# Pool products, early modulation products and output weight splits moved within the attention stage of a two-layer backbone step

## The reference

```python
q, k, v, p = split(h @ w_in)                       # 4 heads of 2 x 64, pool input p of 512
s = einsum('bhqjd,bhkjd->jbhqk', qblk, k) * 64 ** -0.5
pr = softmax(s, axis=-1)
a = pr[0] - lam * pr[1]                            # differential attention
o = einsum('bhqk,bhkv->bhqv', a, v)
o = o * rsqrt(mean(o * o) + LN_EPS) * norm_g * (1 - lam_init)
mixed = einsum('btgc,gcd->btgd', centred_window_means(p), pool_w)   # 4 groups
out = concat([o, mixed * pool_scale]) @ w_out
x = LN(alpha * x + gate * out)
```

## Time and profile before

| | |
|---|---|
| median of 3 runs | 1456.0 us (1455.67 to 1458.06) |
| the profiled execution, its own time | 1456.0 us |
| its span, first to last instruction | 1454.4 us |
| TensorE busy | 1373.7 us, 94% of the span |
| TensorE weight loads | 1129.6 us, 78% |
| VectorE busy | 887.6 us, 61% |
| ScalarE busy | 725.8 us, 50% |
| mean granted TensorE clock | 0.985 |

### The profile page before, as it was taken

The page is one execution under the profiler, slowest core; times in us unless marked ns, Lnnn a source line. Parts: engine busy times, 40 slices in busy tenths (PEclk is TensorE's granted clock), DMA queues, the critical chain, the costliest instruction groups (busy, mean ns, idle before and its releaser), DMA issues.

```text
span 1454.4 us, 20841 instructions
## 1 busy us (share of the span) xinstructions
PE 1373.7 (94%) x6944; PEld 1129.6 (78%) x6944; DVE 887.6 (61%) x1184; ACT 725.8 (50%) x1123; POOL 213.5 (15%) x280
## 2 busy tenths in 40 slices
PE   6999889999999999998889899999999999999986
PEld 2766468999999879986567588888888888888874
DVE  1325557363333484224876697655555999999977
ACT  1323555322333353323434685445445888888863
POOL 1010000070000004103420644100000700000110
PEclk9999999999999999999989999999999999999998
DMA  9786673369443424446655699766656999999991
GB/s 349 227 306 226 217 231 113 116 238 330 131 127 122 129 58 133 116 173 222 235 196 176 235 381 352 253 191 217 206 180 184 369 369 366 371 367 371 370 371 61
DMA packets 254102, 341.24 MB, mean 235 GB/s; under 512 B 15886, under 2 KB 209708, under 8 KB 253900
## 3 DMA queue, kind: packets, MB, share of 16 engines
q1 hardware_dynamic: 241354, 299.55, 62.8%
q0 software_dynamic: 12432, 40.70, 7.5%
q10 hardware_dynamic: 242, 0.01, 0.0%
HBM read 318.13 MB, written 21.02 MB: 233 GB/s over the span
## 4 chain that ended last, share of the span: by engine, by line
PE 80%; DVE 8%; DMA 3%; ACT 3%; issue 3%; SPq 2%; POOL 0%; DVEq 0%; ACTq 0%
PE PS L2259 24%; PE PS L508 14%; PE PS L2266 11%; PE PS L484 7%; PE PS L485 7%; PE PS L486 7%; PE PS L630 2%; SPq L2040 1%; DMA BIG<-in_moe_w_gu 1%; PE PS L2231 1%; DMA BIG<-in_poolm 1%; PE PS L655 1%; DMA raw<-in_w_in_a 1%; ACT whi L2057 1%; DMA raw<-in_ada_w 1%
## 5 line engine op out<-in xcount | busy, mean ns | idle before, releaser
L460 DVE TENSOR_TENSOR wlo<-raw,whi 128x1024 fp32r<-128x1024 f32 x130 | 168.1, 1319 | 225.5 <-ACT whi L457 225.2
L2061 DVE TENSOR_TENSOR wlo<-BIG,whi 128x1024 fp32r<-128x1024 f32 x192 | 239.2, 1263 | 72.7 <-ACT whi L2057 69.7
L2057 ACT ACTIVATE whi<-BIG 128x1024 fp32r<-128x1024 f32 x192 | 202.5, 1059 | 70.6 <-PE PS L2259 37.6
L2259 PE MATMUL PS<-whi,Hh 128*128 128x512 f32 x560 | 223.1, 398 | 0.8 <-DVE Hl L2129 0.7
L2259 PE MATMUL PS<-whi,Hl 128*128 128x512 f32 x560 | 218.7, 391 | 0.0
L2259 PE MATMUL PS<-wlo,Hh 128*128 128x512 f32 x560 | 218.1, 389 | 0.0
L484 PE MATMUL PS<-Hh,whi 128*128 128x384 f32 (+1 forms) x624 | 208.8, 335 | 4.2 <-DVE Hl L794 2.2
L486 PE MATMUL PS<-Hh,wlo 128*128 128x384 f32 (+1 forms) x624 | 207.8, 333 | 0.0
L485 PE MATMUL PS<-Hl,whi 128*128 128x384 f32 (+1 forms) x624 | 207.6, 333 | 0.0
L2061 DVE TENSOR_TENSOR wlo<-raw,whi 128x1024 fp32r<-128x1024 f32 x144 | 177.4, 1243 | 46.3 <-ACT whi L2057 44.7
L2057 ACT ACTIVATE whi<-raw 128x1024 fp32r<-128x1024 f32 x144 | 152.2, 1059 | 55.7 <-PE PS L2266 30.2
(11 more groups left out here) (399 smaller groups left out, 1955.7 us busy)
## 6 DMA issues: line engine op xcount, KB each, us to landing
raw<-in_moe_w_gu SPq DMA_DIRECT2D x224, 256.0 KB, 6.8
BIG<-in_moe_w_gu SPq DMA_DIRECT2D x224, 256.0 KB, 6.5
raw<-in_ada_w SPq DMA_DIRECT2D x96, 512.0 KB, 5.1
BIG<-in_moe_w_down SPq DMA_DIRECT2D x80, 512.0 KB, 8.0
raw<-in_ffn_w_gu SPq DMA_DIRECT2D x44, 512.0 KB, 4.8
raw<-in_w_in_c SPq DMA_DIRECT2D x32, 512.0 KB, 4.0
raw<-in_moe_w_down SPq DMA_DIRECT2D x32, 512.0 KB, 8.0
scr_tok<-BIG POOLq DMA_DIRECT2D x28, 512.0 KB, 9.9
```

Source lines behind the costliest of these rows:

```text
L460: self.eng.tensor_tensor(wlo[:, s, :], raw[:, s, :], whi[:, s, :].bitcast(f32), ALU.subtract).then_inc(lo_made, 1)
L2057: act.activation(whi[:, slot(v), :], moe_raw(v), ACT.Copy).then_inc(hi_made, 1)
L2061: dve.tensor_tensor(wlo[:, slot(v), :], moe_raw(v), whi[:, slot(v), :].bitcast(f32), ALU.subtract).then_inc(lo_made, 1)
L2259: last = pe.matmul(PS[:, 6 * b + c % 2, :], lhs, wt[:, s, 512 * k:512 * k + 512], start=(q == 0 and k == 0 and lhs is h and wt is whi), st ...
```

## The change

Nothing is computed otherwise; instructions are moved within their engines' orders.

- PE: the pool mix of group g leaves its place after the scores of unit g + 2 and stands directly behind the transposes turn(g), one step ahead of those scores.
- All engines: the last two of the 24 modulation units go from iteration 10 to iteration 9; the aftermath of the last vector goes from iteration 11 to iteration 10, on PE ahead of turn(9), on ACT ahead of the copy of it (ACT has no work in it), on DVE to the end of the iteration.
- PE, end: value(10) goes ahead of the first output tile, the waits for pool and modulation ahead of it too, and sum(10) goes between tile 0 and tile 2.
- DVE: the low halves of the output weights. The first stood in iteration 11 behind the mix of unit 10 and now closes iteration 10; the second stood in iteration 12 together with the third and now closes iteration 11; the rest stay.
- ACT's order of high halves is as it was.

```diff
-        ADA_EARLY_AT = [0, 2, 2, 2, 2, 2, 4, 2, 4, 2, 2, 0]
+        ADA_EARLY_AT = [0, 2, 2, 2, 2, 2, 4, 2, 4, 4, 0, 0]
@@ pe_mixer0
                 if i < LASTU:
                     pe_attn_scores(pe, i)
-                if 2 <= i < 6:
-                    pe_pool_mix(pe, i - 2)
                 if i >= 2:
                     pe_attn_value(pe, i - 2)
-                if i not in (5, NU - 2):
+                if i != 5:
                     ada.units(ADA_EARLY_AT[i])
...
-                if i in (5, NU - 2):
+                if i == 5:
                     ada.units(ADA_EARLY_AT[i])
-                if i == LASTU:
-                    ada.after_last(range(KT))
+                if i == NU - 2:
+                    ada.finish()
                 if i >= 1:
                     pe_attn_turn(pe, i - 1)
+                if 1 <= i < 5:
+                    pe_pool_mix(pe, i - 1)
             pe_attn_scores(pe, LASTU)
-
+            pe_attn_value(pe, NU - 2)
+
+            pe.wait_ge(pool_s, 4)
             pe.wait_ge(pool_lo, 4)
+            pe.wait_ge(modc_read, cols_before(EARLY[1]))
+            pe.wait_ge(gate_made, 8)
             pe.wait_ge(lo_made, split_count(U_OUTA))
             k = OUTA_ORDER[0]
             n_tile(pe, U_OUTA, 0, Hh[:, k, :], Hl[:, k, :], True, False)
-            pe_attn_value(pe, NU - 2)
-            pe.wait_ge(pool_s, 4)
-            pe.wait_ge(modc_read, cols_before(EARLY[1]))
-            pe.wait_ge(gate_made, 8)
+            pe_attn_sum(pe, NU - 2)
             n_tile(pe, U_OUTA, 2, Hh[:, k, :], Hl[:, k, :], True, False)
-            pe_attn_sum(pe, NU - 2)
             pe_attn_turn(pe, LASTU)
@@ dve_mixer0
                 if i == LASTU:
-                    sp_.upto(U_OUTA)
                     dve_attn_max(dve, LASTU)
                     dve_attn_norm(dve, LASTU - 2)
...
-                if i == LASTU:
-                    ada.after_last(range(KT))
-                if i > LASTU:
-                    sp_.upto(U_OUTA + (2, 3, 4)[i - NU])
+                if i == NU - 2:
+                    ada.finish()
+                if i >= LASTU - 1:
+                    sp_.upto(U_OUTA + (0, 1, 2, 3, 4)[i - LASTU + 1])
```

## The result

The changed kernel takes 1463.96 us (median of 7 runs, 1459.16 to 1464.3) where the kernel before takes 1455.67 us (7 runs beside it, 1454.2 to 1458.06). The ratio is 1.0054, with an interval of 1.0043 to 1.0066: by that ratio 7.9 us slower, between 6.3 and 9.6 (the two medians differ by 8.3). The forecast was 1460.3 with a range from 1457.0 to 1463.3; the sign is right, the size too small, and the time lies outside the range.

The account below looks back on a forecast made before the run. No engine bounds the attention stage, hand-offs do; TensorE bounds the output product behind it. 1456.0 + 2.4 (pool) + 1.9 (modulation units and low halves, at output tile 1) = 1460.3 us, clock net 0; 8-in-10 range 1457.0 to 1463.3.

Parts of the forecast that it names:

- pool, to value(3): Pool iterations up to unit 3's value product: +2.4 us, lower end 1.2, upper end 3.4.
- value(3) to value(9): Between the value products of units 3 and 9: value(9) 3.0 us late, waiting for norm(8).
- value(9) to tile 1: From unit 9's value product to output tile 1: 3.0 us late at its start, +1.9 at its end.
- tile 1 to end: Behind output tile 1: all rows shifted by one amount, 4.3 us later.
- part 2: Modulation units and aftermath one iteration earlier: turn(9) and ACT's first high half 0.6 us late; 0.8 come back in iteration 11.
- the sentence that left transfers out: Attention stage: transfers not the limit, DMA share 0.65, no PE gap found ending with a load; later PE gives more time.
- The pool: Each middle group's mix waits for ACT's copy, 1.97 us after the sum, uncovering 0.9 us of scores.
- group 3 with its window: Last pool group: its scores at 0, upper end +0.5; its window product's wait for DVE's scaling +0.25, ends 0 and 0.5.
- The low halves: End of iteration 10: DVE's first low half waits for ACT's high half, delaying norm(8); value(9) 3.0 us late.
- The end order: Attention's end: value(9) at about 189.7, output tile 1 at 198.2; value(10) costs nothing, norm(10) by sum(10) hidden by 0.3 us.
- The clock: Same fall to 1.2 GHz and 1.5 us price, ahead of value(9) and not at tile 1: net 0.
- The rival with the clock: Long pool pauses and value(9)'s each end with a clock fall, at most two costing 1.5 us each: 1463.3 us, chance 0.17.

Follow-up runs that it names:

- a3_ada: Kernel before with only the two modulation units and the aftermath one iteration earlier on all engines: 1455.6 us, ratio 1.0014 to before.
- b2_low_back: Changed kernel with DVE's low halves put back where they were: 1460.25 us, ratio 1.0042 to the kernel before.
- b3_copy_first: Changed kernel with ACT's copy pT ahead of the reciprocal root: 1462.51 us, ratio 1.0065 to the kernel before.
- b1_clock: Changed kernel with 14 products without use on PE in the gap ahead of value(9): 1459.58 us, ratio 1.0039 to the kernel before.
- a4_units_back: Changed kernel with the two modulation units back in iteration 10, aftermath still in iteration 10: 1462.81 us, ratio 1.0064 to the kernel before.
- d1_units_early: Changed kernel with the two extra modulation units in iteration 7 and not in 9: 1461.85 us, ratio 1.0047 to the kernel before.
- a1_pool: Kernel before with only the pool mix moved ahead of the scores: 1457.67 us, ratio 1.0031 to before.
- a2_low: Kernel before with only DVE's low halves one iteration earlier: 1456.63 us, ratio 1.0022 to before.
- b4_pe_end: Kernel before with only PE's end order changed, value(10) ahead of tile 0 and sum(10) ahead of tile 2: 1455.09 us, ratio 1.0008 to before.
- c1_norm_first: Kernel before with one low half fewer ahead of norm(10) and ACT's fourth high half behind the root: 1453.68 us, ratio 1.0 to before.
- c2_copy_first: Kernel before with ACT's copy pT ahead of the reciprocal root: 1455.23 us, ratio 1.0006 to before.
- c3_both: Kernel before with norm(10) brought forward and ACT's copy pT ahead of the reciprocal root: 1453.19 us, ratio 0.9999 to before.

## Why the prediction was right in sign and too small in size

By the marks, against the prediction's own steps:

| step | predicted | measured |
|---|---|---|
| pool, to value(3) | +2.4 | +3.05 |
| value(3) to value(9) | +3.0 | +5.64 |
| value(9) to tile 1 | -1.1 | +0.78 |
| tile 1 to end | 0 | -1.61 |
| sum | +4.3 | +7.86 |

- **The step that failed** is in part 2, "The modulation weights are in time: the ring asks for them five units ahead and PE is later than before", together with the sentence that left transfers out. The second half is beside the point: a load is requested when PE has used the unit six before it, so a later PE makes it later too. What counts is how long after the request the unit is used, and moving the two last units from iteration 10 to 9 took 3.0 us from that: from 7.97 us (176.43 to 184.40) to 4.96 (179.26 to 184.22, where PE's wait begins). SP's queue, in the kernel before and in the changed one, for the last two modulation loads:

```profile
L440 SPq DMA_DIRECT2D raw<-in_ada_w x2: 328/846/1364, 176.1 to 176.4; - x2
...
DMA to landing us min/median/max: 3.6/5.3/6.9
```
```profile
L440 SPq DMA_DIRECT2D raw<-in_ada_w x2: 328/862/1397, 178.9 to 179.3; - x2
...
  PEld PS L630: 2.4, 1
```

  Before, the slower of the two landed 6.9 us after 176.4, at 183.3, and the products that needed it began at 184.40: about one us to spare, readable ahead of the change. After, the request at 179.3 is due again some 7 us later, and PE stood there until 186.64. It costs 2.4 us, by the wait of PE's weight loads above and by the marks: value(7) to value(8) takes 3.62 us before, 1.0 more with two more units, and 7.04 here. The same sum holds in a3_ada (3.62 + 1.0 + a wait of 2.1 = 6.7), b2_low_back (2.2, 6.84), b3_copy_first (1.8, 6.38) and b1_clock (0.3, 4.93). In the four with the long waits the load's own issue took 1.4 to 1.7 us, in b1_clock 0.43; why an issue is long stays open. The wide scatter of the times is not explained by it: a4_units_back and d1_units_early wait for no load and scatter as widely.
- **The pool** was right in mechanism (a1_pool, and the unchanged 1.97 us) and 0.65 too small. Group 0 cost 0.42, groups 1 and 2 1.06 each, group 3 with its window 0.51. The mix takes 0.84 until scores follow it; I used 0.75, which is to the value product. Behind scores a value product takes 0.1 longer too, and group 3, which I took at 0 with its window at 0.25, cost 0.51 together.
- **The low halves** were right. DVE's idle time ended by ACT's high half, norm(8) behind the low half and a gap of 3.1 us ahead of value(9) all came as written. Undone (b2_low_back) they give value(9) back 2.5 us beside the load's 0.2, alone (a2_low) they cost it 2.42. From value(3) to value(9) it is 2.64 us more than predicted: 2.4 are the load, and the remaining 0.2 was not separated further.
- **The end order** came out in size at full clock: predicted 8.5 us from value(9) to tile 1, 8.46 in b1_clock. That it agrees so closely is in part luck, as value(9) came 0.7 us later there than its norm allowed, which gave DVE and ACT a lead.
- **The clock** was forecast at net 0. It cost up to 2.0 us ahead of tile 1 and saved 1.6 behind it, net +0.4 at most, with a low time three times as long as forecast; that the two nearly cancel is luck. The forecast tied the fall to the longest gap. The runs do not bear that out: b2_low_back has the same 10.2 us with no gap over 1.32 in the 30 us ahead of it, b1_clock fell while the fillers ran, and three variants of the kernel before (b4_pe_end, c1_norm_first, c2_copy_first) fell with no gap over 0.71 within 6 us. What decides where the clock falls and how long it stays low was not found. The rival with the clock gave falls at the pool's pauses. In the changed kernel and its variants with these pauses there were none: 1.00 through pauses of 1.26 to 1.48 us. The one fall near it is in c3_both, 1.8 us behind value(3), and its pauses are no longer than 1.4. The kernel described in the Trainium skill, page "TensorE: Matmul & The Clock Gate", section "HAM oscillation — how this bites in real kernels", waits about 3 to 5 us each time by that page. So its case says nothing of pauses as short as the pool's, and the prediction, which left that length out, took more from it than it gives.

Together: 4.3 + 0.65 (pool) + 2.4 (load) + 0.2 (not separated) + 0.3 (clock and end) = 7.85, against 7.86 measured. The last two terms are what the marks leave over, so the sum has to close; the load and the pool are measured by themselves. The parts done alone are late by 3.06, 4.06, 2.02 and -0.56 at the end, 8.6 in sum, so they nearly add up; the rest, 0.7 us, was not separated, and the clock's low time, which falls at another place in each, is one candidate.

## What to carry to other kernels

When a consumer of streamed data moves earlier, compare for that very buffer the time from its request to its landing with the time to its use; a mean DMA share and "no wait seen" say nothing about the margin, and a request that is triggered by the consumer's own progress is never made early by a late consumer. On an in-order engine a piece of background work belongs behind the instructions that others wait for, and not where its own input is not ready yet: both waits, the input's and the work's, are handed to everything queued behind. A gap in a stage bound by hand-offs can be cover for something: here the same wait, moved one place earlier in PE's order, lost the scores that it had hidden. And a mark that lies behind a stretch of low clock moves with that stretch: look where it lies before a microsecond is put down to an edit (c1_norm_first).

## What the hardware showed that was not expected

- The granted clock's low stretch has neither one place nor one length: 3.4, 6.8, 10.2 or 13.7 us in fourteen profiles of closely related kernels. In the changed kernel it was low for 10.2 us from the 3.14 us gap on, although PE was busy in 7.76 of the 10.20 us shown; with the gap filled with products it was low for 3.4 us. But b2_low_back was low as long (10.2 us, PE busy in 8.96 of them) without any such gap, and in c3_both it fell at 159.50, 1.8 us behind a pause of 1.32 us and nowhere else in the stage.
- The last modulation load before took its queue 1.36 us to issue where its neighbours took 0.33 to 0.43, and landed 6.9 us after its request where the one just ahead took 3.6, both of the same size. The same load took 0.9 to 1.8 us to issue in eleven of the fourteen profiles; in a1_pool and b1_clock the load behind it was the slow one (1.2 and 1.4 us), and in d1_units_early none was.
